# Key lookups from single identity columns, positions ahead of constants, a mask read late

## The reference, cut to what matters

```python
def t5_bucket(rel):
    rel = jnp.maximum(rel, 0)
    relf = jnp.maximum(rel, 1).astype(jnp.float32)
    large = MAX_EXACT + (jnp.log(relf / MAX_EXACT) / math.log(MAX_DISTANCE / MAX_EXACT)
                         * (N_BUCKETS - MAX_EXACT)).astype(jnp.int32)
    large = jnp.minimum(large, N_BUCKETS - 1)
    return jnp.where(rel < MAX_EXACT, rel, large)

bias = rel_bias[t5_bucket(pb[:, :, None] - ps)]    # 32 buckets x 8 heads
```

## Time and profile before

| what | value |
|---|---|
| median of three runs | 1845.69 us |
| the profiled execution's own time | 1845.32 us |
| its span | 1843.5 us |
| TensorE busy | 1814.4 us, 98% |
| VectorE busy | 1277.9 us, 69% |
| ScalarE busy | 963.2 us, 52% |
| GpSimd busy | 203.0 us, 11% |
| DMA moved | 424.09 MB, mean 230 GB/s |

### The profile page before, as it was taken

How to read it: one execution, slowest core, us unless ns; L and a number is a source line. 1 busy time by engine, 2 the same in 40 slices (tenths; PEclk the granted TensorE clock), 3 DMA queues, 4 the chain that set the end, 5 groups by cost and what they waited for, 6 DMA issues and landing times.

```text
span 1843.5 us, 25345 instructions
## 1 busy us (share of the span) xinstructions
PE 1814.4 (98%) x9769; PEld 1478.1 (80%) x9769; DVE 1277.9 (69%) x1779; ACT 963.2 (52%) x1368; POOL 203.0 (11%) x261
## 2 busy tenths in 40 slices
PE   6999999999999999999999999999999999999997
PEld 3568788888888878888988888888888888888886
DVE  6349989998987778658756544488885466665555
ACT  5345565456465446545644644577764445343464
POOL 1000021001000001100000000045440020021001
PEclk9999999999999999999999999999999999999999
DMA  9999879967986976654465565655555555557562
GB/s 357 386 369 353 304 250 334 324 224 231 344 278 231 384 243 222 216 161 151 147 218 184 184 200 187 199 176 167 167 167 198 184 187 178 192 173 261 180 197 92
DMA packets 195155, 424.09 MB, mean 230 GB/s; under 512 B 7392, under 2 KB 12396, under 8 KB 193644
## 3 DMA queue, kind: packets, MB, share of 16 engines
q1 hardware_dynamic: 193228, 414.67, 66.0%
q10 hardware_dynamic: 1824, 8.02, 1.1%
HBM read 418.45 MB, written 4.21 MB: 229 GB/s over the span
## 4 chain that ended last, share of the span: by engine, by line
PE 91%; DVE 4%; DMA 2%; issue 1%; ACT 1%; SPq 0%; DVEq 0%; POOLq 0%; POOL 0%; ACTq 0%
PE acc L770 27%; PE acc L772 26%; PE acc L771 26%; DVE w_lo L2010 1%; DMA raw<-in_w_mod 1%; PE tps L895 1%; PE tps L813 1%; DMA raw<-in_w_in 1%; PE acc L933 1%; PE acc L934 0%; PE acc L935 0%; PE sps L1033 0%; DVE proj L2145 0%; PE sps L1032 0%; DMA proj<-in_positions 0%
## 5 line engine op out<-in xcount | busy, mean ns | idle before, releaser
L2010 DVE TENSOR_TENSOR w_lo<-raw,w_hi 128x1024 fp32r<-128x1024 f32 (+1 forms) x572 | 712.2, 1249 | 449.2 <-ACT w_hi L1386 446.5
L1386 ACT ACTIVATE w_hi<-raw 128x1024 fp32r<-128x1024 f32 (+1 forms) x572 | 599.1, 1051 | 750.0 <-PE acc L772 685.9
L770 PE MATMUL acc<-w_hi,ht_hi 128*128 128x512 f32 (+1 forms) x2272 | 896.9, 395 | 0.8 <-issue 0.8
L772 PE MATMUL acc<-w_hi,ht_lo 128*128 128x512 f32 (+1 forms) x2272 | 881.5, 388 | 0.0
L771 PE MATMUL acc<-w_lo,ht_hi 128*128 128x512 f32 (+1 forms) x2272 | 879.6, 387 | 0.0
L772 PEld LDWEIGHTS acc<-w_hi,ht_lo 128*128 128x128 f32 x2272 | 426.5, 188 | 88.8
L770 PEld LDWEIGHTS acc<-w_hi,ht_hi 128*128 128x128 f32 x2272 | 426.8, 188 | 85.8 <-issue 4.3
L771 PEld LDWEIGHTS acc<-w_lo,ht_hi 128*128 128x128 f32 x2272 | 427.3, 188 | 82.2
L2145 DVE SCALAR_TENSOR_TENSOR proj<-raw,vcol,proj 128x1024 f32<-128x1024 f32 x60 | 80.2, 1338 | 3.8
L2145 DVE SCALAR_TENSOR_TENSOR scr<-raw,vcol,scr 128x1024 f32<-128x1024 f32 x60 | 79.0, 1316 | 4.0
L2842 POOL TENSOR_TENSOR scr<-scr 128x128 f32<-128x128 f32 x56 | 31.0, 586 | 156.8 <-DVE scr L2584 156.8
(11 more groups left out here) (331 smaller groups left out, 1481.6 us busy)
## 6 DMA issues: line engine op xcount, KB each, us to landing
raw<-in_w_in SPq DMA_DIRECT2D x203, 1024.0 KB, 5.1
raw<-in_w_mod SPq DMA_DIRECT2D x64, 1024.0 KB, 5.6
raw<-in_w_out SPq DMA_DIRECT2D x32, 1024.0 KB, 5.2
raw<-in_w_mod SPq DMA_DIRECT2D x44, 512.0 KB, 11.3
raw<-in_w_o SPq DMA_DIRECT2D x16, 1024.0 KB, 5.1
raw<-in_w_ple_gate SPq DMA_DIRECT2D x16, 1024.0 KB, 5.1
raw<-in_w_b_out SPq DMA_DIRECT2D x8, 1024.0 KB, 5.1
raw<-in_w_a_out SPq DMA_DIRECT2D x8, 1024.0 KB, 5.1
```

The costliest lines, as they stand in the source:

```text
L770: pe.matmul(o, hi_m, w_hi[:, slot, u, 0:width], start=start, stop=False)
L772: mm = pe.matmul(o, lo_m, w_hi[:, slot, u, 0:width], start=False, stop=stop)
L1386: act.activation(w_hi[:, x % SPL, :, 0:width], raw[:, j, 2 * (x % halves):2 * (x % halves) + 2, 0:width], ACT.Copy).then_inc(hi_ready, 1)
L2010: dve.tensor_tensor(w_lo[:, x % SPL, :, 0:width], raw[:, j, 2 * (x % halves):2 * (x % halves) + 2, 0:width], w_hi[:, x % SPL, :, 0:width]. ...
```

## The change

- The mask moves to the end of `kst`. ScalarE's queue loads positions first and then `kst` without the mask (239 columns of 495); SyncE loads the mask after the last piece of the front, with a semaphore of its own, for which VectorE waits ahead of `angles()`.
- `key_pick` is gone. GpSimd makes only a 128 x 128 bf16 identity, `ident_b`.
- `spread_keys` takes one column of `ident_b`, broadcast to 32 stationary columns, per key, and writes it to that key's 32 partitions: four products where there was one. Rounds 0 to 15 have eight products of 256 columns, rounds 16 to 23 sixteen of 128.

```diff
-C_MASK = C_ID + P
-C_INV = C_MASK + 2 * P
+C_INV = C_ID + P
...
-C_N = C_TH + SIGNS
+C_MASK = C_TH + SIGNS
+C_N = C_MASK + 2 * P
...
-        key_pick = proj[:, 1, 4096:4096 + P * NB // 2].bitcast(BF16)
-        ident_b = key_pick.rearrange("p (k b) -> p k b", b=NB)[:, :, 0]
+        ident_b = proj[:, 1, 4096:4096 + P // 2].bitcast(BF16)
...
             for g in range(FRONT):
                 first_weights(3, g)
+            sp.dma_start(kst[:, C_MASK:C_N], consts[:, C_MASK:C_N]).then_inc(s_mask, 16)
             free.skip(8 * FRONT)
...
                 for e in range(CH // w):
-                    at = P * (g0 + e)
-                    mm = pe.matmul(key_cols(n)[:, e * w:(e + 1) * w], key_pick[:, at:at + P], b_t, start=True, stop=True)
+                    for key in range(KPG):
+                        pick = ident_b[:, KPG * (g0 + e) + key:KPG * (g0 + e) + key + 1].broadcast_to([P, NB])
+                        mm = pe.matmul(key_cols(n)[NB * key:NB * (key + 1), e * w:(e + 1) * w], pick, b_t, start=True, stop=True)
                 mm.then_inc(keys_spread, 1)
...
-            act.dma_start(kst[:, :], consts).then_inc(s_const, 16)
             act.dma_start(prow_i, positions.partition_broadcast(P)).then_inc(s_pos, 16)
+            act.dma_start(kst[:, 0:C_MASK], consts[:, 0:C_MASK]).then_inc(s_const, 16)
...
                 if l == 0:
                     dve.wait_ge(s_const, 16)
+                    dve.wait_ge(s_mask, 16)
                     angles()
...
             pool.wait_ge(s_const, 16)
-            pool.tensor_copy(key_pick.rearrange("p (k b) -> p k b", b=NB), bc(ident, NB)).then_inc(pick_ready, 1)
+            pool.tensor_copy(ident_b, ident).then_inc(pick_ready, 1)
```

More of the change, by code:

```diff
@@ L126, in constants @@
     k[0, C_SEL] = k[32, C_SEL] = k[64, C_SEL + 1] = k[96, C_SEL + 1] = 1.0
-    k[:, C_TH:C_N] = [-e for e in EDGES[:SIGNS]]
+    k[:, C_TH:C_MASK] = [-e for e in EDGES[:SIGNS]]
     lv = np.zeros((P, 5, P), np.float32)
@@ L335, in build @@
         s_const = sem("s_const")
+        s_mask = sem("s_mask")
         s_x = sem("s_x")
```

## The result

The changed kernel takes 1849.84 us (median of 15 runs, 1848.38 to 1852.89) against 1845.50 us before (15 runs): +4.3 us, ratio 1.0023, 95% interval [1.0016, 1.0030]. It is slower, by slightly more than the 0.2% drawn as the border, to which the prediction gave a chance of 0.12. The forecast was +0.1 us. Run again beside other kernels it took 1849.91 us against 1845.54 us, ratio 1.0027 [1.0018, 1.0036].

The account below looks back on a forecast made before the run. Front taken as a race between DMA bytes and TensorE: 4.6 us of sets and trips, less 1.7 at the start, less 2.8 of waits, gives +0.1 us on the 1845.69 us median: 1845.8 us, range 1844.6 to 1849.8.

Parts of the forecast that it names:

- rival 3: At the start: consts land later and another wait holds the signs, so no early gain; +1.8 us, 1847.5 us, chance 0.18.
- the cover: Front to 130 us: TensorE's DMA waits absorb 2.8 us of delay, DMA backlog 2.9 us; the later decides, +0.1 us.
- the start: First DMAs and signs: positions first, consts split and copy cut start VectorE's product 1.7 us sooner, bounds 1.3 and 2.2 us.
- The sets and trips: Spread products in the rounds: dearer sets 1.5 us, shape trips 3.5 us, VectorE lateness covered -0.4 us; 4.6 us added.
- the term of 8 x 0.21 = 1.7 us: Last eight spread sets: sixteen 32-column loads each take 0.44 us against 0.23 us now.
- Rival 1: Spread products: column groups don't overlap in bf16, sets and trips cost 19.7 us, 15.2 us net; 1860.9 us, chance 0.05.
- The latest landing of consts: At the start: consts, loaded second, land no later than 7.84 us; 7.4 us was taken.
- Its own sign of being wrong: Front: the prediction called itself wrong if DMA's share drops below 1 in 30 to 50 us.
- the prediction's rule: Front: 2.8 us of any TensorE delay vanishes in its own waits for DMA.
- The bytes and the mask: End of front: moving the mask's 0.13 MB behind the weights ends DMA 0.3 us sooner; its late read costs 0.

Follow-up runs that it names:

- e1: Kernel before with only the four products per key group and the small identity copy, old DMA order and mask: +5.1 us against before.
- e2: Kernel before with only the DMA order changed (positions first, consts split, mask late), old copy and wide products kept: +2.9 us against before.
- e9: Kernel before with every wide spread product issued twice, 128 TensorE instructions more: +3.2 us against before.
- e3: Changed kernel with consts (without the mask) loaded first and positions second: +3.4 us against before.
- e5: Kernel before with nearly only the mask read late, consts without it first, old copy and wide products kept: -0.2 us, ratio 1.0000.
- e6: Kernel before with 64 unread two-column products (128 instructions) in TensorE idle time ahead of the signs: +0.3 us against before.
- e4: Changed kernel with spread sets issued two at a time and three modulation slots moved one round ahead, to halve trips: +4.6 us against before.
- e7: Changed kernel with 64 unread two-column products (128 instructions) in TensorE idle time ahead of the signs: +4.5 us against before.
- e8: Kernel before with eight two-column products added per spread set, 384 instructions more, wide products kept: +4.8 us against before.

## Why the prediction came out as it did, step by step

The measured time lies at the very end of the range (1849.84 us, the range was given up to 1849.8), the forecast 4 us below it. That the range reached so far is luck: it was drawn past rival 3, whose condition came true (the early start gives nothing) but whose +1.8 us rests on the same cover as the forecast. Two steps make up the difference, the cover and the start; a third was wrong by two errors that cancel.

**The sets and trips: right in kind, too dear in one term.** Priced: set of eight 0.22 us and 0.13 us for going in, measured 0.33; lookups behind it 0.39 us, measured 0.40; 0.22 us behind a modulation slot, measured 0.22. Off was the set of sixteen: priced at 0.44 us for its loads (0.57 with the trip), measured 0.34: 0.22 us for sixteen products without the trip, so that the term of 8 x 0.21 = 1.7 us was in truth nothing. A 32-column load costs no more than 0.014 us here, since sixteen fit into 0.22 us, and not 0.027. The columns were 4.8 us late; less 1.9 us of halts and 0.1 us at the start that leaves 2.8 us for sets and trips, against 4.6 us in the sum. Rival 1 (groups one after another, +15 us) is refuted, and with it, for this shape, the rule of the Trainium skill, "TensorE: Matmul & The Clock Gate", Part 3, that was weighed there: here the row group is the same, and sixteen loads and products take 0.22 us, no more than the columns alone.

**The halts: missing.** 0.82 + 1.04 = 1.9 us in both profiles. No step of the sum had TensorE's program in it, and no row of before pointed to it; its packets were in the trace all the same.

**The start: most of the 1.7 us did not come.** `bucket_b`, at 17.07 us before, was begun at 17.18 us, and at 16.48 us in the second profile: 0.1 us later and 0.6 us sooner. The latest landing of consts that I allowed was 7.84 us; it was 9.15 and, in the second profile, 8.44 us. In second place half of consts took 7.8 us (7.1 in the second profile), where all of it took 4.4 in first place. Neither packets nor bytes decide but what stands ahead: positions are slow by themselves, 6.3 us even in first place (5.4 in the second profile), and consts land behind them. That VectorE's cast is stretched by GpSimd's copy was named and left unused; e1 shows that it is worth 0.8 us at the first sign, in the old order; in the changed kernel consts land too late for it.

**The cover: the step that failed.** The prediction let 2.9 us of delay vanish in DMA backlog and 2.8 us in TensorE's own waits, and called the later of the two the result. Its own sign of being wrong came: DMA's share fell to 0.82 in 40 to 50 us. In the kernels whose columns were 3.0 to 5.4 us late the medians are +2.9 to +5.1 us; less 2.8 us, as the prediction has it, they would be +0.2 to +2.6 us. The cleanest case is e2, with no new instruction: 3.0 us at the columns, 2.8 us at 272 us, +2.9 us in the median, where the prediction's rule gives 0.2. Only e9 comes near the rule, +3.2 against +2.6 us.

The reading that fits is that the two are no separate absorbers but one loop. A slot is refilled when TensorE has read it, and TensorE's later waits for DMA are made of those refills. They were 2.8 us in all before. They don't simply vanish for a late TensorE: in the first profile of the changed kernel they were 0.6 us, and its delay fell from 4.8 us at the columns to 3.3 us at 272 us; in the second they were 4.5 us, and the delay grew from 4.1 to 5.3 us:

```profile
PE tps L897 <- DMA proj<-in_w_mod: 2.0, 2, 1.2
PE tps L897 <- DMA raw<-in_w_mod: 2.0, 2, 1.2
...
PE tps L897 <- DMA scr<-in_w_mod: 0.5, 1, 0.5
```

e3 (0.7 us of waits, 4.2 to 2.4 us) and e1 (4.6 us, 4.1 to 5.0 us) repeat the two cases. So a part of the cover acts in some executions and in others the waits add to the delay; which of the two happens, and why, is open. The backlog was taken as 8.0 us less 5.1 us of an unhindered transfer, but the refills before that one, at 21 to 31 us, have less: in e2 DMA was short at 29 us already. The full DMA share before the change told that the loop just held, not that it had slack.

**The bytes and the mask.** The mask cost nothing that can be told (e5), and VectorE reads it without a wait, as forecast. The 0.3 us that its bytes were to give back is below what any run here can show.

Put together: 4.6 us became 2.8 of sets and 1.9 of halts, nearly the same sum. The columns were 4.8 and 4.1 us late, and the medians are +4.3 and +4.4 us. Without the cover the prediction's own numbers would have given 2.9 - 0.3 = +2.6 us; the 1.7 us missing to +4.3 are as much as the start was to give. How much of a delay arrives varies from one execution to the next by some 2 us (3.3 and 5.3 us at 272 us for the changed kernel), and a median takes the middle of that.

No run beats the kernel before: the best, e5, is level with it. Its front moves its bytes at full rate from 10 us on, so a gain ahead of 42 us would have to go into the first refills; e6, whose columns came 0.7 us sooner, ended at +0.3 us.

## What to carry to other kernels

Where a producer refills a slot only after the consumer has read it, a delay of the consumer and the backlog of the producer are one quantity: follow the refills in order and look for the first that comes late, instead of taking the backlog of one of them as cover. And look at the granted clock of each stretch before you compare two profiles: by the estimates above e3 and e4 lost to it about what their edits had won. Before splitting a product into several small ones, count its instructions as well as its array time; here four concurrent 32-column products took no more array time than one wide one, apart from the trip. The landing of a small transfer was set here by what stood ahead of it in its queue more than by its size (119.5 KB: 4.1 us in first place, 7.8 us in second).

## What the runs showed of the hardware that was not expected

- GpSimd's fp32 to bf16 copy (3.60 us) and a VectorE operation on SBUF get in each other's way: beside the copy a 0.43 us product took 3.83 us (e2), a 0.30 us cast 1.15 us (e5) and 1.27 us (before), each ending just after the copy, which took its 3.60 us every time. The Trainium skill has this in "SBUF — State Buffer", SBUF: two separate sides, as an exclusive lock on a shared port pair; the rows agree.
- Entering and leaving the 32-column shape cost 0.11 us each in bf16, and four such products at once cost what one wide one costs (0.11 us for 256 columns).
- 384 more TensorE instructions in 27 us brought halts of 0.8 to 2.4 us, each ending 1.3 to 1.5 us behind a 16 KB program packet; at the same two places of the program in the changed kernel's two profiles and e1, only at the first in e3.
- Behind the halts of 1.37, 1.81 and 2.39 us (e3, e7, e4) the granted clock fell, to 0.83 to 0.89 in the lowest stretch of 10 us; behind the halts of 0.77 to 1.10 us in the changed kernel, e1 and e8 it stayed at 1.00.
- One weight transfer of 1 MB took 7.6 to 7.9 us in four profiles and 5.0 to 5.8 us in the other eight at the same place; the cause is open.
